# Expert layer of a two-block transformer: the tokens of each group gathered in the middle of the group before it

## The reference

```python
def ec_moe(h, router, w1, w3, w2):
    b_, n, _ = h.shape
    cap = EC_CAPACITY * n // N_EXPERTS
    aff = jax.nn.softmax(jnp.einsum('bld,de->ble', h, router).astype(F32), axis=-1)
    gate, idx = lax.top_k(jnp.swapaxes(aff, 1, 2), cap)
    bidx = jnp.arange(b_)[:, None, None]
    xe = h[bidx, idx]
    hid = jax.nn.silu(jnp.einsum('becd,edf->becf', xe, w1)) * jnp.einsum('becd,edf->becf', xe, w3)
    ye = jnp.einsum('becf,efd->becd', hid, w2) * gate[..., None].astype(h.dtype)
    return jnp.zeros_like(h).at[bidx, idx].add(ye)
```

## Time and profile before

| | us |
|---|---|
| median of 3 runs | 5403.37 |
| lowest, highest | 5393.2, 5405.93 |
| the profiled execution | 5405.11 |
| its span in the trace | 5403.3 |
| granted TensorE clock, mean | 0.937 of full speed |

### The profile page before, as it was taken

The page is one execution under the profiler, slowest core; times in us unless marked ns, Lnnn a source line. Parts: engine busy times, 40 slices in busy tenths (PEclk is TensorE's granted clock), DMA queues, the critical chain, the costliest instruction groups (busy, mean ns, idle before and its releaser), DMA issues.

```text
span 5403.3 us, 80212 instructions
## 1 busy us (share of the span) xinstructions
PE 4835.4 (89%) x33872; PEld 2948.3 (55%) x33872; DVE 2127.8 (39%) x3904; ACT 1301.5 (24%) x2400; POOL 426.1 (8%) x386
## 2 busy tenths in 40 slices
PE   8899999988988969979887997999998997999999
PEld 2466666676554544453233554544777554544777
DVE  2455555553354451031112236363333236363333
ACT  0233333332222210010001133231222123232222
POOL 0011111110231230000000000010000000010000
PEclk9899999998989979989998997999999997999999
DMA  6000000001101022127997110113221210113221
GB/s 247 27 18 18 18 18 18 4 5 45 39 32 47 16 100 115 70 91 324 419 418 293 71 53 20 59 55 126 106 94 52 85 53 20 48 59 130 109 94 47
DMA packets 70701, 494.63 MB, mean 92 GB/s; under 512 B 8771, under 2 KB 9027, under 8 KB 29251
## 3 DMA queue, kind: packets, MB, share of 16 engines
q1 hardware_dynamic: 70342, 489.49, 23.4%
HBM read 468.47 MB, written 21.00 MB: 91 GB/s over the span
## 4 chain that ended last, share of the span: by engine, by line
PE 75%; DVE 9%; issue 8%; DMA 5%; ACT 2%; POOL 1%; SPq 0%; DVEq 0%; POOLq 0%; PEldq 0%; ACTq 0%; PEld 0%
PE ps L224 72%; DMA upper<-in_ew 4%; PE ps L227 3%; DVE upper L235 2%; ACT upper L282 1%; DVE upper L243 1%; DVE upper L259 1%; DVE lower L235 1%; POOL upper L3250 1%; DVE lower L243 1%; DVE upper L251 1%; DVE upper L239 1%; DMA lower<-in_ada 0%; ACT lower L282 0%; DVE upper L255 0%
## 5 line engine op out<-in xcount | busy, mean ns | idle before, releaser
L224 PE MATMUL ps<-lower 128*128 128x512 f32 (+10 forms) x6512 | 1958.2, 466 | 94.4 <-issue 25.1
L224 PEld LDWEIGHTS ps<-lower 128*128 128x128 f32 (+3 forms) x6512 | 1010.2, 198 | 852.3 <-issue 668.3
L224 PE MATMUL ps<-upper 64*64 64x64 f32 (+7 forms) x14224 | 913.6, 261 | 148.5 <-DVE upper L251 42.9
L282 ACT ACTIVATE upper<-ps 128x512 f32<-128x512 f32 (+6 forms) x963 | 445.6, 483 | 2094.8 <-PE ps L224 1432.3
L224 PEld LDWEIGHTS ps<-upper 64*64 64x64 f32 (+4 forms) x14224 | 653.9, 150 | 466.1 <-issue 247.4
L224 PE MATMUL ps<-lower,upper 64*64 64x64 f32 (+6 forms) x7216 | 818.4, 326 | 73.7 <-DMA lower<-in_ew 27.5
L224 PE MATMUL ps<-rounded 128*128 128x512 f32 x3072 | 719.8, 396 | 30.6 <-DVE rounded L235 23.1
L224 PEld LDWEIGHTS ps<-rounded 128*128 128x128 f32 x3072 | 583.1, 190 | 166.5 <-ACT rounded L282 26.3
L224 PEld LDWEIGHTS ps<-lower,upper 64*64 64x64 f32 (+3 forms) x7216 | 415.0, 146 | 415.0 <-issue 360.0
L224 PE MATMUL ps<-upper,lower 128*128 128x512 f32 (+4 forms) x1200 | 507.3, 571 | 16.3 <-DVE lower L243 5.6
L282 ACT ACTIVATE upper<-upper 128x768 f32<-128x768 f32 (+10 forms) x615 | 323.6, 531 | 677.8 <-POOL upper L3250 144.4
(11 more groups left out here) (78 smaller groups left out, 2112.1 us busy)
## 6 DMA issues: line engine op xcount, KB each, us to landing
lower<-in_ew SPq DMA_DIRECT2D x144, 1024.0 KB, 12.0
upper<-in_ew SPq DMA_DIRECT2D x48, 1024.0 KB, 13.7
lower<-in_b0f SPq DMA_DIRECT2D x16, 2048.0 KB, 8.1
lower<-in_b1f SPq DMA_DIRECT2D x16, 2048.0 KB, 7.7
lower<-in_ada SPq DMA_DIRECT2D x12, 2048.0 KB, 9.4
lower<-in_wrkv SPq DMA_DIRECT2D x8, 1728.0 KB, 7.3
lower<-in_b0g SPq DMA_DIRECT2D x8, 1536.0 KB, 6.6
gad<-upper SPq DMA_DIRECT2D x48, 256.0 KB, 2.0
```

Of the source, the lines that this page charges most:

```text
L224: return self.e.matmul(out, lhsT, rhs, start=start, stop=stop)
L282: self.e.activation(out, in_, func, bias=bias, scale=scale, accum_out=accum).then_inc(line.up(*event), 1)
```

## The change

`gather` is now made for one group at a time, 128 places. Group 0's stands before the groups; that of group g + 1 stands in group g, behind the transposes of f = 1 and ahead of the `PT` transposes. It takes one pair of PSUM banks: ScalarE copies one bank (`kk` 0 to 3), VectorE the other (4 to 7), each as soon as it is written. `XE` and `YE` become three buffers used in rotation, so the copies of group g wait for `combine(g - 3)`. Since `h2` is now read up to group 6, `acc` gets memory of its own. `P` is built in two pieces: for experts 0 and 1 first (event "P", 0), then for the other 14.

```diff
-    hA = m(4096)
-    b.acc = v3(hA, 1024)
+    m(4096)
...
-    b.XE = m(8192).rearrange("p (g k s) -> p g k s", g=8, k=8)
-    b.YE = b.XE.rearrange("p g k s -> p g (k s)")
+    b.acc = v3(m(4096), 1024)
+    b.YE = [m(1024) for _ in range(3)]
+    b.XE = [v3(e, 128) for e in b.YE]
...
+    def gather(g):
+
+        use = ("gather", g)
+        ps = banks.take(use, 2)
+        pe.wait_ge(M.dve, "P", min(g, 1))
+        for kk in range(8):
             for i in range(4):
-                last = pe.mm(ps, k.h2[:, i, 128 * kk:128 * kk + 128], b.P[:, i, 512 * hf:512 * hf + 512], i == 0, i == 3)
-            last.then_inc(M.pe.up(*use), 1)
-            banks.give(use, (M.act, M.dve)[kk % 2], *use)
+                last = pe.mm(ch(ps, kk), k.h2[:, i, 128 * kk:128 * kk + 128], b.P[:, i, 128 * g:128 * g + 128], i == 0, i == 3)
+            if kk % 4 == 3:
+                last.then_inc(M.pe.up(*use, kk // 4), 1)
+        banks.give_each(use, (M.act, *use), (M.dve, *use))
...
-    gather(0, range(8))
+    gather(0)
     for g in range(8):
-        if g in (0, 4):
-            pe.wait_ge(M.act, "gather", g // 4, 6)
-            pe.wait_ge(M.dve, "gather", g // 4, 7)
+        pe.wait_ge(M.act, "gather", g)
+        pe.wait_ge(M.dve, "gather", g)
...
-            if g == 0:
-                gather(1, range(4 * f, 4 * f + 4))
-            elif f == 0:
+            if g and f == 0:
                 combine(g - 1)
+        if g < 7:
+            gather(g + 1)
...
-    for i in range(4):
-        v.tt(M.dve, v3(b.P[:, i, :], 64), bc1(c["iota"], 16), bc2(b.slt[:, 16 * i:16 * i + 16], 64), ALU.is_equal,
-             *(("P",) if i == 3 else ()))
+    for z, (e0, e1) in enumerate(((0, 2), (2, 16))):
+        for i in range(4):
+            v.tt(M.dve, v3(b.P[:, i, 64 * e0:64 * e1], 64), bc1(c["iota"], e1 - e0),
+                 bc2(b.slt[:, 16 * i + e0:16 * i + e1], 64), ALU.is_equal, *(("P", z) if i == 3 else ()))
```

More of the change, by code:

```diff
@@ L2113, in combine @@
                 last = pe.mm(ps[:, 512 * n:512 * n + 512], b.PT[:, g, 128 * i:128 * i + 128],
-                             b.YE[:, g, 512 * n:512 * n + 512], True, True)
+                             b.YE[g % 3][:, 512 * n:512 * n + 512], True, True)
             last.then_inc(M.pe.up(*use), 1)
@@ L2129, in pair @@
             last.then_inc(M.pe.up(*use, z), 1)
[L2131 removed]
+    gather(0)
     for g in range(8):
[L2133 to L2135 removed]
+        pe.wait_ge(M.act, "gather", g)
+        pe.wait_ge(M.dve, "gather", g)
         for f in range(2):
             for name in ("ew1", "ew3"):
[L2138 removed]
+                pair((name, g, f), b.XE[g % 3])
                 banks.give((name, g, f), M.dve, "glu", g, f)
@@ L2196, in moe_vector, with gather @@
     v.copy(M.dve, b.slt, k.pair("place")[:, 0:64], "place")
-    for i in range(4):
-        v.tt(M.dve, v3(b.P[:, i, :], 64), bc1(c["iota"], 16), bc2(b.slt[:, 16 * i:16 * i + 16], 64), ALU.is_equal,
-             *(("P",) if i == 3 else ()))
[L2201 to L2205, removed]
+    for z, (e0, e1) in enumerate(((0, 2), (2, 16))):
+        for i in range(4):
+            v.tt(M.dve, v3(b.P[:, i, 64 * e0:64 * e1], 64), bc1(c["iota"], e1 - e0),
+                 bc2(b.slt[:, 16 * i + e0:16 * i + e1], 64), ALU.is_equal, *(("P", z) if i == 3 else ()))
+    def gather(g):
+        if g > 2:
+            v.wait_ge(M.pe, "combine", g - 3, 3)
+        v.wait_ge(M.pe, "gather", g, 1)
+        v.copy(M.dve, b.XE[g % 3][:, 4:8, :], v3(k.pair(("gather", g))[:, 512:1024], 128), "gather", g)
     def combine(g):
@@ L2233, in moe_vector @@
             v.wait_ge(M.pe, "ew2", g, n, 1)
-            v.ts(M.dve, b.YE[:, g, 512 * n:512 * n + 512], k.pair(("ew2", g, n)), b.gs[:, g:g + 1], MUL, event=("down", g, n))
+            v.ts(M.dve, b.YE[g % 3][:, 512 * n:512 * n + 512], k.pair(("ew2", g, n)), b.gs[:, g:g + 1], MUL, event=("down", g, n))
     combine(7)
@@ L2254, in moe_scalar, with gather @@
     a.act(M.act, b.lg, b.lg, AF.Exp, "lexp")
[L2256 to L2262, removed]
+    def gather(g):
+        if g > 2:
+            a.wait_ge(M.pe, "combine", g - 3, 3)
+        a.wait_ge(M.pe, "gather", g, 0)
+        a.copy(M.act, b.XE[g % 3][:, 0:4, :], v3(k.pair(("gather", g))[:, 0:512], 128), "gather", g)
+    gather(0)
     for g in range(8):
```

## The result

| | us |
|---|---|
| before, median (4 runs) | 5403.72 (5393.2 to 5405.93) |
| changed, median (4 runs) | 5371.11 (5369.64 to 5376.22) |
| ratio, changed to before | 0.9945, 95% interval 0.9928 to 0.9962 |
| span of the profiled execution, changed | 5367.8 (before 5403.3) |

The change makes the kernel 32.6 us faster; 28.9 were forecast, and 5371.1 stands beside the predicted 5375.

The account below looks back on a forecast made before the run. The layer was taken to begin bound by TensorE, while loads stand still, and end bound by loads. Terms -24.2 - 18.5 + 5.1 + 11.5 - 2.8 = -28.9 us gave 5375 beside 5403.4; range 5359 to 5392.

Parts of the forecast that it names:

- Start of group 0: Before the groups: P in pieces and a shorter first gather, first product at 2395.4 instead of 2419.67, -24.2 us.
- The narrow record: In each gather, a 128-column matmul with its own weight load takes 0.111 us, a gather 7.1 us.
- S: Gather records run at the Trainium skill's pace, 0.155 us each: 5397 us, no change; chance 0.05.
- B: Weight loads of the gather records run in series, 0.081 us more each: +41, 5416 us; chance 0.04.
- Group 0: 27.6 us of gather go out, 7.1 come in, with 1.9 of waits: 84.7 becomes 66.2, -18.5 us.
- Groups 1 to 6: Each gets a gather, 3.4 us of wait, period 62.2: +5.1 us for the first, +11.5 for the other five.
- Rival D: In the groups with a gather, loads never stand still and periods are 59.9 us: 5361 us; chance 0.14.
- Rival E: In the groups, the gather adds to 52 us of work and 7.8 of waits, period 66.6: +26, 5401; chance 0.07.
- Rival C: Each of seven gathers within groups makes the clock fall, 5.1 us lost a time: +36, 5411 us; chance 0.04.
- group 7, to the last combine: Last group, without a gather and with a fuller ring at its start: 57.1 for 59.9, -2.8 us.
- the law: Weight ring: a stage is ready 9.05 us after the one four before is done, at least 4.99 after its predecessor.
- The latency of 9.05: Weight ring: time from the start of a replacement at 2494.01 to its first stage being there, 9.05 us.

Follow-up runs that it names:

- the repeat: The changed kernel run once more, unedited: layer time 548.1 us against 548.2, device time 5368.0 us.
- the two placements: Changed kernel, next group's gather moved behind the combine in f = 0 (layer time 573.5 us) or into "ew2" (536.9 us).
- within "ew2": Changed kernel, next group's gather moved from behind f = 1 to between n = 0 and n = 1 of ew2: layer time 536.9 us, device time 5355.93.

## Why the prediction was right, step by step

Times from the first transposes; the prediction's absolute ones were made for a layer that begins at 2343.8.

- **Start of group 0.** Predicted 51.6, measured 51.9. P in pieces gave 3.6 of the 3.8 us claimed (the run with P in one piece), the first gather took 10.8 where 10.6 were forecast.
- **The narrow record.** Predicted 0.111 us, a gather of 7.1. Measured 7.15 from start to start (2428.99 to 2436.14), 0.112. The nearest row carried this, and the rivals S and B fall. Scaled from what the Trainium skill (TensorE: Matmul & The Clock Gate, Back-to-back issue gap) gives for 128 columns, an estimate, it would have been 9.9; the trace does not agree, and the measurement decides.
- **Group 0.** Predicted 66.2, measured 64.7. The term of 1.9 for the waits was too high: 0.39 at 2424.01. In the repeat the wait was 1.92, and a shorter two-column row (8.61) made up for it: 64.6.
- **Groups 1 to 6.** Predicted 62.2 each. The starts of the combines lie 62.5, 61.2, 61.1, 62.3, 62.0 and 61.8 apart, 61.8 in the mean. Taken from the starts of the stages, the waits of groups 2 to 6 are 2.7 us in the mean where 3.4 were forecast, and TensorE's own work is 59.1 where 58.8 were; two small errors that partly cancel. The DMA share over these groups is 0.99 (0.96 forecast, 1.01 before). The run without inner gathers, the doubled ones and the two placements show the reason given, not only the size.
- **What was missed.** From its first product to the next group's, group 1 took 64.5 us, not 62.2. TensorE ran a stage at half clock behind a wait of 2.75 us, 5.35 us instead of 3.65 at 2476.39; the prediction left the clock as it was. In the repeat no stage of group 1 ran at half clock, and it took 61.3. What makes the clock fall there was not tried.
- **Rival D** (no standing still, 59.9) did not come in this kernel. Its period did come within "ew2" (60.3 in the mean) and with ten slots (59.9), by the place and the depth and not by faster refills. Rival E (waits whole) would have kept 45.6 us of waits; there were 19.2. Rival C (the clock falls behind gathers) did not come: 1.00 in the middle stretches.
- **The sum.** -28.9 forecast, -31.7 in the layer. The device time moved by 32.6, with small moves outside the layer of the size that any two runs have. Term by term, each group from its first product to the next group's:

| term | forecast | before, changed | measured |
|---|---|---|---|
| start of group 0 | -24.2 | 75.9, 51.9 | -24.0 |
| group 0 | -18.5 | 84.4, 64.7 | -19.7 |
| group 1 | +5.1 | 58.9, 64.5 | +5.6 |
| groups 2 to 6 | +11.5 | 301.2, 309.1 | +7.9 |
| group 7, to the last combine | -2.8 | 59.5, 58.1 | -1.5 |

Every term has the right sign. The largest error is that of groups 2 to 6: 1.9 us of it are their shorter periods, and 1.6 are the one longer period of the kernel before (61.5), which the prediction took to stand in both kernels and which the changed kernel's trace does not show.

Where the law was off in the experiments, it was mostly too favourable where loads set the pace (527 for 531.9 and 530.3, 531 for 536.9) and too harsh where the ring ran short (605 for 598.8). Two misses have a cause of their own: 598 for 594.7 counts from the changed kernel, whose group 1 had a stage at half clock that the kernel with doubled gathers did not have, and 518 for 521.0 took the loads' 59.9 for the period where TensorE's own work needs 60.2. The latency of 9.05, read at one place, is the number I trust least in it (below); that it explains both signs was not shown.

## What to carry to other kernels

Where a ring of buffers feeds a consumer that is nearly as slow as the loads, the amounts alone do not set the time; it also matters where the consumer's pauses stand (here a pause is a time in which it uses no tile of the ring). Work put into a pause in which the ring is already full costs nearly its whole length, and the same work where the ring is short costs little: 41.6 and 5.0 of 50 us here. An early start gains only if no long pause follows it. Follow ring and consumer by hand with three numbers from the trace (a stage, a load, the time from a freed slot to its refill) before moving work, and try the depth of the ring.

## What the runs showed of the hardware

- The time from a freed slot to a ready stage is not constant within one kernel. From the first issue of a refill to the start of the fourth stage, less three times 4.98, the changed kernel's trace has 7.66, 9.14, 8.90, 7.56, 7.49, 8.70, 8.42 and 8.21 us for its groups; the row of before from which I took 9.05 gives 9.1 by the same measure. Other runs lie between 7.6 and 9.8. What decides was not tried.
- Records of 128 columns in 32-bit floats, each with its own 128x128 weight load, take 0.112 us where a quarter of a 512-column record (0.43) is 0.107. Records of two columns, which leave little but the weight load, take 0.1 at full clock. So load and matmul run side by side and at 128 columns last about equally long; I read from this, and no run tried it, that records narrower than 128 columns would gain next to nothing.
- A row of 64 two-column records took 10.41, 8.61 and 11.61 us in three traces of nearly the same program, as the clock fell to 1.2 GHz at another place in it: 3.5, 5.5 and 2.2 us after its start. In all twelve traces with the whole row, that of before among them, the clock fell 2.2 to 5.5 us into it and stayed down for 6.8 to 13.7 us; in the two in which it was broken up, it stayed at full speed in group 0. So the row as a whole brings this fall. It is not the only one: the stage of group 1 had another, of 3.4 us.
